# Feed-forward operands built one combination at a time on VectorE, with the last norm's sums, the reload of the accumulator and the weight splits before the last down group moved

## The reference

```
def _rmsnorm(x, g):
    y = x32 * lax.rsqrt(jnp.mean(x32 * x32, axis=-1, keepdims=True) + EPS)
    return y * g
def _swiglu(xn, w_gu, w_down):        # w_gu 1024 x 5632, w_down 2816 x 1024
    gu = xn @ w_gu
    g, u = jnp.split(gu, [D_FF], axis=-1)
    return (jax.nn.silu(g) * u) @ w_down
x = x + mixer(rmsnorm(x, norm1_g))
x = x + _swiglu(rmsnorm(x, norm2_g))
y = rmsnorm(x, final_g)
```

## Time and profile before

| | |
|---|---|
| median of 3 runs | 2779.88 us (2779.03 to 2780.5) |
| profiled execution, its own time | 2776.99 us |
| its span, first to last instruction | 2775.1 us |
| mean granted TensorE clock | 0.991 |
| busy in the span | PE 97%, DVE 75%, ACT 49%, POOL 9% |

### The profile page before, as it was taken

How to read it: one execution, slowest core, us unless ns; L and a number is a source line. 1 busy time by engine, 2 the same in 40 slices (tenths; PEclk the granted TensorE clock), 3 DMA queues, 4 the chain that set the end, 5 groups by cost and what they waited for, 6 DMA issues and landing times.

```text
span 2775.1 us, 39261 instructions
## 1 busy us (share of the span) xinstructions
PE 2693.0 (97%) x15404; PEld 2659.8 (96%) x15404; DVE 2068.4 (75%) x2738; ACT 1363.8 (49%) x1849; POOL 255.9 (9%) x423
## 2 busy tenths in 40 slices
PE   8999999999999999999899999999999999999995
PEld 7999999999999999999899999999999999999995
DVE  7868787788878877887766676688667688676666
ACT  6743484358436743663454344454434356344443
POOL 2000101020101011101410000031000030000000
PEclk9999999999999999999999999999999999999998
DMA  7453567646665656475464444456444454544443
GB/s 238 133 183 116 191 224 259 197 159 230 240 210 174 242 208 231 163 238 190 159 200 134 144 136 138 130 165 216 133 144 131 143 154 156 197 137 138 134 132 98
DMA packets 148550, 481.84 MB, mean 174 GB/s; under 512 B 16752, under 2 KB 34416, under 8 KB 148368
## 3 DMA queue, kind: packets, MB, share of 16 engines
q1 hardware_dynamic: 106224, 345.21, 38.5%
q0 software_dynamic: 31632, 117.66, 12.3%
q10 hardware_dynamic: 10512, 16.46, 2.0%
HBM read 414.75 MB, written 64.51 MB: 173 GB/s over the span
## 4 chain that ended last, share of the span: by engine, by line
PE 74%; DVE 13%; issue 6%; ACT 4%; DMA 2%; POOL 0%; SPq 0%; DVEq 0%; ACTq 0%; POOLq 0%
PE ps L678 74%; ACT wring L852 2%; DVE wring L1646 2%; DVE xacc L1637 1%; DVE main L1779 1%; DVE ga L1767 1%; DVE tmp L1314 1%; DVE tmp L1765 1%; DMA wraw<-dwm 1%; DMA xacc<-x1s 1%; DVE work L1603 1%; ACT work L1118 1%; ACT sq L883 0%; ACT wextra L852 0%; DVE work L1605 0%
## 5 line engine op out<-in xcount | busy, mean ns | idle before, releaser
L678 PE MATMUL ps<-ycomb,wring 128*128 128x346 f32 (+1 forms) x5544 | 886.5, 322 | 11.3 <-DVE main L1779 7.2
L678 PEld LDWEIGHTS ps<-ycomb,wring 128*128 128x128 f32 x5544 | 883.8, 189 | 12.2 <-DVE wring L1646 7.6
L1646 DVE TENSOR_TENSOR wring<-wraw,wring 128x1024 fp32r<-128x1024 f32 (+1 forms) x571 | 696.8, 1221 | 249.5 <-ACT wring L852 247.0
L852 ACT ACTIVATE wring<-wraw 128x1024 fp32r<-128x1024 f32 (+1 forms) x571 | 591.5, 1038 | 503.5 <-PE ps L678 486.1
L678 PE MATMUL ps<-xhi,wring 128*128 128x416 f32 (+1 forms) x1728 | 480.2, 354 | 14.2 <-DVE wring L1646 8.9
L678 PE MATMUL ps<-hcomb,wring 128*128 128x346 f32 (+1 forms) x2772 | 454.1, 324 | 19.6 <-DVE wring L1646 9.7
L678 PEld LDWEIGHTS ps<-hcomb,wring 128*128 128x128 f32 x2772 | 444.2, 190 | 27.5 <-issue 14.6
L678 PE MATMUL ps<-yhi,wring 128*128 128x416 f32 x1568 | 429.9, 351 | 2.8 <-DVE ylo L1318 2.7
L678 PEld LDWEIGHTS ps<-xhi,wring 128*128 128x128 f32 x1728 | 327.4, 189 | 19.7 <-issue 11.8
L678 PE MATMUL ps<-xlo,wring 128*128 128x416 f32 (+1 forms) x864 | 306.1, 354 | 0.0
L678 PEld LDWEIGHTS ps<-yhi,wring 128*128 128x128 f32 x1568 | 294.3, 188 | 5.7 <-ACT yhi L905 3.3
(11 more groups left out here) (239 smaller groups left out, 2732.4 us busy)
## 6 DMA issues: line engine op xcount, KB each, us to landing
wraw<-dwm SPq DMA_DIRECT2D x247, 512.0 KB, 3.9
wraw<-sgu SPq DMA_DIRECT2D x132, 512.0 KB, 3.3
wraw<-graw SPq DMA_DIRECT2D x99, 512.0 KB, 3.5
wraw<-sdn SPq DMA_DIRECT2D x48, 512.0 KB, 3.6
pbuf<-graw POOLq DMA_DIRECT2D x22, 1024.0 KB, 7.2
sgu<-pbuf POOLq DMA_DIRECT2D x22, 1024.0 KB, 6.1
wraw<-fused SPq DMA_DIRECT2D x40, 512.0 KB, 3.3
wraw<-draw SPq DMA_DIRECT2D x36, 512.0 KB, 3.7
```

What stands on the lines that cost most here:

```text
L678: mm = nc.tensor.matmul(out, wt[:, c * P:(c + 1) * P], x, start=(first and q == 0), stop=(last and q == 2), skip_group_check=chain)
L852: A(ring(n)[:, 0, 0:c], wraw[:, n % RAW, 0:c], ACT.Copy, scale=cst[:, PSC, name[2]:name[2] + 1] if name[0] == "w" else 1.0).then_inc(w_hi, 1)
L1646: V.tensor_tensor(ring(n)[:, 1, 0:c], wraw[:, n % RAW, 0:c], ring(n)[:, 0, 0:c].bitcast(f32), SUB).then_inc(w_lo, 1)
```

## The change

The seven products are reordered (1, 2, 6, 5, 7, 3, 4 instead of 1, 5, 6, 3, 7, 2, 4), and the chains follow. The operands are built by combination: each is one instruction over four channel tiles on ACT and one on DVE (CORDER gives the order), the three plain quarters come first through work[11:15], and the differences are four instructions on DVE (T1 to T4) instead of twelve on POOL. TensorE waits for each combination just before its first use. The tables BESIDE_B, BESIDE_O, BESIDE_GU and BESIDE_DN say beside which step each is made; combination 6 is made inside the slice's first gate-up step. The squares of the last block's second norm move from the o steps into gate-up step 0, the matmul with ones moves before product k = 6, the reciprocal from product 1 to product 0 of step 1, and the finished tiles from steps 1 and 2 (k = 2 to 4, 0 to 4) to steps 1 and 2 (k = 1 to 4, 0 to 1). The accumulator's stores and loads wait by halves. The narrow slots of the last down group get four places instead of three, in the same memory (wlast), and the splits of the last pair's final release come earlier in the programs of ACT and DVE.

```diff
-PROD = (1, 5, 6, 3, 7, 2, 4)
-ROLE = {1: 0, 6: 0, 7: 0, 4: 0, 5: 1, 3: 1, 2: 2}
+PROD = (1, 2, 6, 5, 7, 3, 4)
+ROLE = {1: 0, 6: 0, 7: 0, 4: 0, 2: 1, 5: 2, 3: 2}
-BUILD = {1: 1, 3: 2, 5: 3}
-TAKE = {0: 0, 2: 1, 4: 2, 6: 3}
-REBUILD = {3: 0, 6: 1, 9: 2, 12: 3}
+FINISH = {(1, 1): (0,), (1, 2): (1,), (1, 3): (2,), (1, 4): (3,), (2, 0): (4, 5), (2, 1): (6, 7)}
+CORDER = (0, 5, 1, 4, 2, 3, 6)
+DIFFS = ("T1", "T3", "T2", "T4")
+BESIDE_B = {1: (0,), 3: (5,), 5: (1,)}
+BESIDE_O = {2: ("T1", "T3"), 3: ("T2", 4), 4: (2,), 5: (3,), 7: ("T4",)}
+BESIDE_GU = {2: (0,), 4: (5,)}
+BESIDE_DN = {1: (1,), 4: ("T1", "T3"), 5: ("T2", 4), 7: (2,), 8: (3,), 11: ("T4",)}
...
+def ring_places():
+    last, places, before = [-1] * 16, [], []
+    for n in range(NS):
+        each = 3 if slot_width(n) == 768 else 4
+        spans = [range(each * q, each * q + each) for q in range(4 if each == 3 or n < NARROW else 3)]
+        held = [max(last[u] for u in span) for span in spans]
+        q = held.index(min(held))
...
+            def plain_quarters(s):
+                if s:
+                    pool.wait_ge(a_lo, 7 * s)
+                quarter(s, 0, 0, 11, y_in[0])
+                pool.wait_ge(a_lo, 7 * s + 1)
+                quarter(s, 1, 0, 11, y_in[0])
+                pool.wait_ge(a_lo, 7 * s + 2)
+                quarter(s, 1, 1, 11, y_in[0])
...
-                    if p == k == 0:
-                        pe.wait_ge(a_hi, 16 * (s + 1))
-                        pe.wait_ge(a_lo, 16 * (s + 1))
                     c = COMBO[prod]
+                    if p == 0:
+                        pe.wait_ge(a_hi, 7 * s + CORDER.index(c) + 1)
+                        pe.wait_ge(a_lo, 7 * s + CORDER.index(c) + 1)
...
+            def operand_lo(s, c):
+                w, q = TH[s], CORDER.index(c)
+                dve.wait_ge(a_hi, 7 * s + q + 1)
+                V.tensor_tensor(ycomb[:, c, 1, :, 0:w], work[:, CFROM[c]:CFROM[c] + 4, 0:w],
+                                ycomb[:, c, 0, :, 0:w].bitcast(f32), SUB).then_inc(a_lo, 1)
...
                 V.tensor_tensor(work[:, 6, 0:w], work[:, 10, 0:w], work[:, 5, 0:w], SUB).then_inc(h_diff, 1)
+                early = p == PAIRS - 1
+                if early:
+                    for q in splits_after(SLOT[("gu", s, p, 6)]):
+                        split_lo(q)
                 dve.wait_ge(h_hi, 4 * n + 2)
                 V.tensor_tensor(hl[:, 2:5, :], work[:, 3:6, 0:w], hh[:, 2:5, :].bitcast(f32), SUB).then_inc(h_lo, 1)
-                for q in splits_after(SLOT[("gu", s, p, 6)]):
-                    split_lo(q)
+                if not early:
+                    for q in splits_after(SLOT[("gu", s, p, 6)]):
+                        split_lo(q)
```

More of the change, by code:

```diff
@@ L204 @@
 NARROW = SLOT[("b", NB - 1, 0)]
-PLACE = [n % (RING if n >= NARROW else RING + 1) for n in range(NS)]
-PREV = [max([m for m in range(max(0, n - 9), n) if PLACE[m] == PLACE[n]], default=-1) for n in range(NS)]
+def ring_places():
[5 more added lines that the diff above has]
+        q = held.index(min(held))
+        places.append(q)
+        before.append(held[q])
+        for u in spans[q]:
+            last[u] = n
+    return places, before
+PLACE, PREV = ring_places()
 RELEASE = list(itertools.accumulate(PREV, max))
@@ L500, in _ @@
             sp.wait_ge(state_stored, 16)
-            sp.wait_ge(y_stored, 16 * KT * (NT - 1))
+            for q in range(2):
+                sp.wait_ge(y_stored[q], 16 * 4 * (NT - 1))
             sp.wait_ge(y_sent, 16 * KT)
@@ new lines, in quarter @@
+            def quarter(s, kh, h, first, landed):
+                cols = slice(TO[s] + h * TH[s], TO[s] + h * TH[s] + TH[s])
+                pool.dma_start(work[:, first:first + 4, 0:TH[s]],
+                               ys[4 * kh:4 * kh + 4, :, cols].rearrange("k p c -> p k c")).then_inc(landed, 16)
+            def plain_quarters(s):
[6 more added lines that the diff above has]
+                quarter(s, 1, 1, 11, y_in[0])
```

271 lines of the change are left out of this document (150 added, 121 removed).

## The result

| | before | after |
|---|---|---|
| median of 5 runs, us | 2779.88 (2777.62 to 2780.5) | 2751.76 (2748.8 to 2754.09) |
| ratio of the times, 95% interval | | 0.9903 (0.9892 to 0.9914) |
| profiled execution: its own time, span | 2776.99, 2775.1 | 2748.8, 2747.0 |
| mean granted TensorE clock | 0.991 | 0.995 |

A forecast was written before the change was run, and what follows sets the result against it. TensorE bounds the kernel, busy 2693.0 of 2775.1 us. Terms 12.0 + 5.2 + 9.9 - 2.7 - 5.7 - 3.4 = 15.3 us off 2776.99 give 2761.7; with 2.9 for the median, 2765 us, range 2751 to 2775.

The forecast's parts named there:

- The last down group: Last down group of each slice: waits of 9.6 us before become 15.3 us after, a loss of 5.7 us.
- The middle of the group: Last down group, slots 4 and 5: VectorE falls behind, four places cover most; 0.6 us of waiting per slice, bounds 0 and 3.
- the low parts: Start of the last down group: three splits now precede the last low part, and TensorE stands 1.8 us.
- Moving the reload: First down group of slices 1 and 2: last finished tile 11 us earlier covers waits of 2.50 and 3.88 us; gain 9.9 us.
- First product of slices 1 and 2: First product of slices 1 and 2: only T4's split may be late, 0.3 us each; gain 5.2 us.
- The estimate of 3.6 us: Quarter for combination 5 before k = 6: the page's fit gives 3.6 us, no wait, and about 2.6 us less time.
- The reciprocal: Step 1 of slices 1 and 2: reciprocal ahead of a split brings a new wait of 1.35 us each; loss 2.7 us.
- Moving the differences: Last down group: four differences put 6.4 us per slice on VectorE, nearly free as POOL's subtractions had cost it 10.5 us.
- The clock: Behind eight new waits of 1.35 to 2.1 us: two clock falls of 1.7 us, loss 3.4 us, bounds 0 and 14.
- The output projection: Last block's output projection and first product: waits of 11.2 us shrink to 1.0, plus 1.8 of clock; gain 12.0 us.
- the one that ends at 2750: Rival: start of the last down group costs no more than before, clock holds; 28 to 31 us won, 2750; chance 0.16.
- The slower rival: Rival: quarters of 692 KB land late; from 10 us on the kernel is slower by over 0.2%, at 11 us 2789; chance 0.06.

The follow-up runs named there:

- norm_late: The changed kernel with the next block's norm in the mixer put back one output-projection step; 2757.36 us, ratio to before 0.9930.
- norm_early: The kernel before with only the mixer's norm moved one output-projection step earlier; 2771.59 us, ratio to before 0.9979.
- four_moved: The changed kernel with combination 3 before 2, combination 0 sooner, finished tiles and reciprocal at old places, ring rotation shifted; 2737.35 us, ratio to before 0.9855.
- splits_behind: The changed kernel with the splits of the last pair's final release put back behind the low parts; 2753.63 us, ratio to before 0.9907.
- finish_late: The changed kernel with finished tiles and reciprocal at their old places, the reload still by halves; 2745.27 us, ratio to before 0.9888.
- c3_first: The changed kernel with combination 3 made one slot ahead of combination 2, so the last quarter is requested sooner; 2744.36 us, ratio to before 0.9881.
- pool_busy: The changed kernel with twelve extra GpSimd subtractions between the mixed quarters and the last one in slices 0 and 1; 2756.04 us, ratio to before 0.9919.
- reload_whole: finish_late with the two halves of stores and reload waited for as one; 2757.67 us, ratio to before 0.9934.
- sums_in_o: The changed kernel with squares and sums of the last block's second norm back beside the output projection; 2756.41 us, ratio to before 0.9924.

## Why the forecast was right in direction and 13 us off

Faster was right, and so were most mechanisms. From profile to profile the forecast had 15.3 us won, and 28.2 came. That the median still lies in the range, 0.8 us above its lower end, is partly luck: 6 us came from an edit that the forecast did not have, and steps that were off both ways made up for each other. What each step held:

- **The missed edit.** "Start-up, the four norms of the mixer and the last norm behind the final product are the same code in both kernels" was false. The full diff has the mixer's edit, and I read past it; the section on the reference says just as wrongly that the mixer is not touched. Between the two profiles it is 4.6 us of waits and 1.7 us of clock, 6.3 us. norm_late and norm_early confirm the waits, and their times (7.5 and 5.8 us) fit the sum. The clock's part may as well have stayed away, as six of the twelve kernels show.
- **The last down group.** Forecast 15.3 us for three groups, measured 5.2 + 4.3 + 1.3 = 10.8, so 4.5 us less. The failing step is "The first narrow slot now takes a place that is free only after product k = 5, not k = 4", which I read from slice 0 and used for all three. ring_places() gives the slots of slices 1 and 2 a place that is free after k = 4; four_moved gives slice 0 that too, and 1.8 us go (2.06 + 1.07 to 0.12 + 0.51 + 0.68). Within slice 0 the terms were near: 1.35 for 1.5, 1.52 for 1.8. The middle of the group waits 1.01 and 1.00 us in slices 0 and 1, for 0.6. The step behind it, the low parts ("Now there are three, 0.9 us each: 1.8 more"), from which the forecast had TensorE stand 1.8 us in each slice, was mis-sized: it waits 1.30 us for them in slice 0 and 0.68 in the others, and splits_behind shows that the sooner splits cost 0.7 us at the start of the group in slice 0 and win 0.5 in each of the others.
- **Moving the reload.** The forecast left 0.66 us of these two waits; 0.38 and 1.32 are left. "The last finished tile moves [...] That covers 2.50 and 3.88 us" gave the sooner tiles as the cause and gave nothing to the split into halves, which is in the diff too. finish_late shows that the halves cover the waits without the sooner tiles; undone with the tiles at their old places they cost 0.0046 or 12.8 us (7.5 of waits and 5.5 of clock behind them). The estimate above says that the sooner tiles alone might have covered them as well, which no run tests; so the cause that the step named is one of two, and not refuted. Its size was off: the last store stands 21.8 us ahead of the first addition in the changed kernel and 14.3 in finish_late, 7.5 us sooner and not 11. And it had no price, where the sooner tiles cost about 1 us in slice 2 and the reciprocals' 2 us. Before, the loads waited 4.53 us for all eight stores; I read past the idle time in that row.
- **First product of slices 1 and 2.** "0.3 us each" was mis-sized: 1.88 and 1.71. I gave the quarter for T4 no time of its own in the sum; it lands 5.8 and 6.4 us after the request. c3_first removes both. For combination 5's quarter 5.0 us was near: requested at 1761.01, copied by ScalarE from 1765.92, 4.9 us (5.1 in slice 1). The estimate of 3.6 us from the Trainium skill, page DMA: Bandwidth & Descriptors, section Anatomy of one DMA, is not borne out: the trace has 4.9 to 6.4 us, while weights stream beside it.
- **The reciprocal.** The mechanism was right, 1.35 us forecast and 1.08 and 1.06 measured; back at its old place the waits are 0.14 and 0.12.
- **Moving the differences.** "Nearly free" holds: the group's narrow splits take 0.95 us in the changed kernel, and pool_busy brings their 1.28 us back. But "the gain is the cover of the fourth place" fell: without it the time is the same, since the late quarter takes up the difference, and only in four_moved is it worth something, 2 to 5 us by waits, spans and ratios.
- **The clock.** Forecast two falls, 3.4 us; the profile of after shows none at the new waits. That is partly luck: splits_behind has a fall behind a wait of 1.81 us at one of these places. The step also counted eight new waits where the prediction's own list has ten.
- **The output projection** came as forecast, 1.5 us left of 11.2 instead of 1.0.

Together: 6.3 + 4.5 + 3.4 for the clock + 0.6 for the reciprocals - 3.0 for T4 - 1.0 for the reload - 0.5 = 10.3 of the 12.9 us between the two sums. Of the other 2.6, some 2.1 lie before the first product on ycomb, which starts 18.06 us sooner (1386.09 to 1368.03) where the terms have 6.3 + 9.7; 0.5 of them are there 53 us into the span already, in the start-up. What made the rest isn't placed. Of the rivals, the one that ends at 2750 is nearest in number, but only half in mechanism: the groups do cost a little more than before (10.8 against 9.6), and what makes up for it is an edit that no rival had. The slower rival's point was right in kind (quarters on the path one to one) and far from its threshold: 4.9 us for combination 5's, 6.4 for T4's, against 10.

## What to carry to other kernels

When a producer waits for all of a group of stores before it reloads, try to split the wait before moving the work: here two semaphores for one cover the reload with the work at its old place, 7.5 us of waits and about 13 us of time, while finishing the work sooner made a weight slot late. When one diff holds two edits for one wait, test each without the other, or the cause stays open. Read the whole diff for edits in stages that the summary doesn't name. A place in a rotating buffer has to be looked up in each repetition, since the rotation need not come round alike. A wait that a buffer's extra place removes can come back at the next late transfer; test such a place again once that transfer is early.

## What the runs showed of the hardware that I had not expected

The granted clock does not follow the length of a wait near 2 to 3 us. Ten us (columns as in the earlier trace rows) behind a wait of 3.01 us in finish_late:

```profile
1819.80:1829.80 10.00, 9.95 (x63) 9.95 (x64) 7.49 (x8) 5.60 (x7) 0.00 (x0) 1.00 0.50 160
```

Behind 2.02 us in reload_whole:

```profile
1820.50:1830.50 10.00, 9.99 (x53) 9.99 (x54) 5.96 (x7) 4.29 (x6) 0.00 (x0) 0.83 0.51 160
```

It stays at 1.00 (2.4 GHz throughout) behind 3.01 us and falls to 0.83 behind 2.02. The shortest wait with a fall behind it is 1.81 us (0.83, splits_behind at 2275.62), while 2.17 us in the same kernel (1823.08) left it at 1.00. The clearest case is the mixer's wait at 1106 us, the same code and the same 2.58 us in both. In finish_late, at 1105.83:

```profile
1105.00:1115.00 10.00, 9.17 (x49) 9.13 (x50) 8.49 (x14) 5.94 (x9) 2.61 (x7) 1.00 0.51 179
```

In four_moved, at 1105.54:

```profile
1105.00:1115.00 10.00, 9.46 (x42) 9.32 (x43) 7.00 (x10) 5.94 (x9) 2.56 (x7) 0.83 0.54 179
```

Twelve profiles have this wait at 2.55 to 2.58 us; six show the fall and six don't. Behind the waits of 3.52, 3.96 and 4.21 us the clock fell for longer: 0.70, 0.74 and 0.71 over 10 us, 2.6 to 3.0 us lost; behind 4.33 us in sums_in_o it was 0.85. Why one wait of 2 or 3 us costs 1.7 us of clock and another nothing stays open. Between two profiles, 1.7 us of clock can so be there or not without any edit.

A 768-column split on VectorE took 1.28 us instead of 0.95 beside GpSimd's subtractions, although they touch other tiles; the additions to xacc in the same stretch kept their pace (872 against 876 ns). And transfers of the same 692 KB took 4.9 us from request to use in one place and up to 6.4 in another.
